# Row gathers of a product-key lookup: six slots and weight units loaded ahead, in place of eight slots

## What is computed

```
q = (xt @ w_q).reshape(T, 8, 2, 128)                 # 8 heads
sc = einsum('thcd,hckd->thck', q, sub_keys)          # 2 x 128 scores a head
s1, i1 = top_k(sc[:, :, 0], 16); s2, i2 = top_k(sc[:, :, 1], 16)
cand = s1[..., :, None] + s2[..., None, :]           # 256 pairs
top_s, top_pos = top_k(cand, 16); gate = softmax(top_s)
idx = take(i1 * 128 + i2, top_pos)                   # 16 experts a token and head
hid = gelu(einsum('tkd,td->tk', u[idx], xt), approximate=False)
out = einsum('tk,tkd->td', gate * hid, v[idx])
```

## Time and profile before

| | |
|---|---|
| three runs, median (lowest to highest) | 2395.85 us (2390.09 to 2397.31) |
| the profiled execution, and its span | 2390.07 us, 2388.0 us |
| TensorE busy | 2096.7 us, 88% |
| VectorE busy | 1732.6 us, 73% |
| ScalarE busy | 789.3 us, 33% |
| GpSimd busy | 574.8 us, 24% |
| moved by DMA | 726.83 MB, mean 304 GB/s |
| granted TensorE clock, mean | 0.985 |
| chain that ended last | DMA 22%, TensorE 23%, VectorE 14%, issue 11% |

### The profile page before, as it was taken

The page is one execution under the profiler, slowest core; times in us unless marked ns, Lnnn a source line. Parts: engine busy times, 40 slices in busy tenths (PEclk is TensorE's granted clock), DMA queues, the critical chain, the costliest instruction groups (busy, mean ns, idle before and its releaser), DMA issues.

```text
span 2388.0 us, 26690 instructions
## 1 busy us (share of the span) xinstructions
PE 2096.7 (88%) x9124; PEld 1365.8 (57%) x9124; DVE 1732.6 (73%) x3737; ACT 789.3 (33%) x1479; POOL 574.8 (24%) x520
## 2 busy tenths in 40 slices
PE   8999999999999889887778779999888988787777
PEld 8998889989877444432322226978544432222224
DVE  6455664558766887878887776656878787878786
ACT  4335653346574221211211116344312121211114
POOL 0000000000101334444444330000434444443430
PEclk9999999999999999999999999999999999999999
DMA  7554325544325999999999995534899999999995
GB/s 264 180 187 168 139 106 179 191 176 168 124 92 192 421 420 416 411 411 420 409 417 416 408 409 220 198 139 172 363 419 420 419 415 419 404 416 420 399 420 209
DMA packets 101354, 726.83 MB, mean 304 GB/s; under 512 B 11632, under 2 KB 11888, under 8 KB 13424
## 3 DMA queue, kind: packets, MB, share of 16 engines
q0 software_dynamic: 74016, 539.00, 54.9%
q1 hardware_dynamic: 25200, 181.41, 21.0%
q10 hardware_dynamic: 2016, 4.89, 0.6%
HBM read 724.21 MB, written 1.05 MB: 304 GB/s over the span
## 4 chain that ended last, share of the span: by engine, by line
PE 23%; DMA 22%; DVE 14%; issue 11%; ACT 2%; POOL 1%; DVEq 0%; POOLq 0%; ACTq 0%
PE bank L2023 23%; DMA arena<-in_uv,expert 22%; DVE arena L1897 3%; DVE arena L1951 2%; POOL arena L677 1%; DVE arena L1870 1%; DVE top_i L1848 1%; DVE arena L1840 1%; DVE top_i L1838 1%; DVE arena L1874 1%; DVE top_v L1843 0%; DVE top_v L1835 0%; DVE sel_s L1851 0%; DVE sel_i L1876 0%; ACT w_hi L730 0%
## 5 line engine op out<-in xcount | busy, mean ns | idle before, releaser
L2023 PE MATMUL bank<-arena 128*128 128x512 f32 (+4 forms) x2416 | 1068.6, 575 | 248.9 <-DVE arena L1897 245.1
L2023 PEld LDWEIGHTS bank<-arena 128*128 128x128 f32 (+2 forms) x2416 | 415.9, 193 | 812.9 <-DVE arena L1897 522.5
L677 POOL DMA_INDIRECT arena<-in_uv,expert x512 | 564.1, 1102 | 1090.1 <-PE bank L2023 657.4
L1951 DVE SCALAR_TENSOR_TENSOR arena<-arena,xn 128x1024 f32<-128x1024 f32 x512 | 626.8, 1224 | 240.3 <-DMA arena<-in_uv,expert 221.5
L1268 DVE TENSOR_TENSOR lw_rounded<-lw,w_hi 128x2048 fp32r<-128x2048 f32 x157 | 362.0, 2306 | 198.6 <-ACT w_hi L730 195.4
L1163 ACT ACTIVATE act_h<-hid 128x1 f32<-128x1 f32 x512 | 103.6, 203 | 1044.5 <-DVE arena L1951 1044.1
L2023 PE MATMUL bank<-xT_hi,w_hi 128*128 128x256 f32 x1320 | 415.5, 315 | 5.5 <-DVE xT_lo L1313 5.5
L730 ACT ACTIVATE w_hi<-lw 128x2048 fp32r<-128x2048 f32 (+1 forms) x177 | 320.7, 1819 | 237.9 <-PE bank L2023 224.0
L2023 PE MATMUL bank<-xT_hi,lw_rounded 128*128 128x256 f32 x1320 | 374.9, 284 | 0.0
L2023 PE MATMUL bank<-xT_lo,w_hi 128*128 128x256 f32 x1320 | 374.7, 284 | 0.0
L2023 PEld LDWEIGHTS bank<-xT_hi,w_hi 128*128 128x128 f32 x1320 | 253.9, 192 | 30.6 <-issue 29.6
(11 more groups left out here) (258 smaller groups left out, 1529.1 us busy)
## 6 DMA issues: line engine op xcount, KB each, us to landing
lw<-in_units SPq DMA_DIRECT2D x169, 1024.0 KB, 4.8
arena<-in_uv,expert POOLq DMA_INDIRECT x512, 12.4
wide<-in_wide POOLq DMA_DIRECT2D x2, 1024.0 KB, 8.9
gain<-in_gains ACTq DMA_DIRECT2D x4, 512.0 KB, 9.4
wide<-in_units SPq DMA_DIRECT2D x2, 1024.0 KB, 7.1
h<-in_x SPq DMA_DIRECT2D x2, 512.0 KB, 4.2
arena<-in_ret_consts ACTq DMA_DIRECT2D x1, 1024.0 KB, 5.2
out<-xn SPq DMA_DIRECT2D x2, 512.0 KB, 2.6
```

Source lines behind the costliest of these rows:

```text
L677: nc.gpsimd.indirect_dma_start(out=rows_uv[:, slot, :], out_offset=None, in_=table, in_offset=bass.IndirectOffsetOnAxis(ap=expert[par][:, ...
L1951: V.scalar_tensor_tensor(rows_uv[:, slot, 0:D], rows_uv[:, slot, 0:D], 1.0, xn[:, tile, :], ALU.mult, ALU.mult, accum_out=hid[par][:, k:k ...
L2023: return nc.tensor.matmul(o, lhsT, rhs, start=start, stop=stop, **more)
```

## The change

SLOTS is 6. The memory of `rows_uv` keeps its eight blocks; in each layer two of them (0 and 1 in the first, 4 and 5 in the second) hold the units head+3 and head+4, the query weights of heads 2 and 3, and the gathers rotate over the other six. These two units are loaded right behind the first query's unit, with semaphores of their own, and their remainder is written in place. The other units keep the ring, but in another order of issue: head+2, head+5, head+7, head+6, head+8, head+9, each behind the unit that held its ring slot before. On VectorE every diagonal follows its own dot, after both top-k steps; AT_ONCE goes. The first six gathers find free slots in place of the first eight.

```
-SLOTS = 8
+SLOTS = 6
+BLOCKS = 8
+UNIT_BLOCKS = ((0, 1), (4, 5))
+ROW_BLOCKS = [[b for b in range(BLOCKS) if b not in blocks] for blocks in UNIT_BLOCKS]
-AT_ONCE = 12
...
-LOADS = {u: sum(v not in WHOLE for v in range(u % RING, u + 1, RING)) for u in range(UNITS)}
+BLOCK_OF = {first + 3 + i: UNIT_BLOCKS[layer][i] for layer, first in enumerate((A_PEER0, A_PEER1)) for i in range(2)}
+LOADS = {u: sum(v not in WHOLE and v not in BLOCK_OF for v in range(u % RING, u + 1, RING)) for u in range(UNITS)}
...
-        rows_uv = region(at, "rows_uv", SLOTS, 2 * D)
+        rows_uv = region(at, "rows_uv", BLOCKS, 2 * D)
+        def row_slot(s):
+            return rows_uv[:, ROW_BLOCKS[s // (ROWS * TOPK)][s % SLOTS], :]
+        def unit_of(u):
+            return rows_uv[:, BLOCK_OF[u], :] if u in BLOCK_OF else lw[:, u % RING, :]
+        def low_of_unit(u):
+            return arena_rounded[:, BLOCK_OF[u] * 2 * D:(BLOCK_OF[u] + 1) * 2 * D] if u in BLOCK_OF else w_lo[:, u % RING, :]
...
                 load_units(head, head + 1, 1)
-                load_units(head + 2, first)
-                sp.wait_ge(row_landed[SLOTS - 3], 16 * (layer + 1) * (ROWS * TOPK // SLOTS))
+                for i in range(2):
+                    sp.dma_start(rows_uv[:, UNIT_BLOCKS[layer][i], :], units_d[head + 3 + i]).then_inc(block_loaded[i], 16)
+                for u, before in ((head + 2, head - 2), (head + 5, head - 3), (head + 7, head - 1), (head + 6, head + 2), (head + 8, head + 1),
+                                  (head + 9, head + 5)):
+                    sp.wait_ge(lw_used, before + 1)
+                    load_unit(u, u % RING)
+                last = (layer + 1) * ROWS * TOPK - 3
+                sp.wait_ge(row_landed[last % SLOTS], 16 * (last // SLOTS + 1))
...
-                            slot = k % SLOTS
+                            s = done + (2 * pair + par) * TOPK + k
                             pool.wait_ge(slot_free, done + SLOTS * layer + (2 * pair + par) * TOPK + k + 1)
-                                out=rows_uv[:, slot, :], out_offset=None, in_=table,
+                                out=row_slot(s), out_offset=None, in_=table,
...
-                            at_once = row == ROWS - 1 and k > AT_ONCE
-                            if at_once:
-                                assert n is None
-                                spread(row * TOPK + k - 1, par, k - 1)
-                            dve.wait_ge(row_landed[slot], 16 * (layer * ROWS * 2 + 2 * row + k // SLOTS + 1))
+                            dve.wait_ge(row_landed[s % SLOTS], 16 * (s // SLOTS + 1))
                             if n is not None:
                                 picked(row + 1, n)
-                            V.scalar_tensor_tensor(rows_uv[:, slot, 0:D], rows_uv[:, slot, 0:D], 1.0, xn[:, tile, :], ALU.mult, ALU.mult,
+                            V.scalar_tensor_tensor(row_slot(s)[:, 0:D], row_slot(s)[:, 0:D], 1.0, xn[:, tile, :], ALU.mult, ALU.mult,
                                                    accum_out=hid[par][:, k:k + 1]).then_inc(dot_done, 1)
                             n = next(ahead, None) if k >= start else None
-                            if k >= 1 and not at_once:
-                                if n is not None:
-                                    picked(row + 1, n)
-                                spread(row * TOPK + k - 1, par, k - 1)
-                                n = next(ahead, None) if k >= start else None
+                            if n is not None:
+                                picked(row + 1, n)
+                            n = next(ahead, None) if k >= start else None
+                            spread(row * TOPK + k, par, k)
                             if k == 10:
                                 weigh(row + 1, 1 - par)
                             beside(slots + par * TOPK + k)
-                        spread(row * TOPK + TOPK - 1, par, TOPK - 1)
...
-                    mm(bank[b][:, :], zeros, consts[:, 0:BANK], True, True).then_inc(slot_free, SLOTS // 4)
+                    mm(bank[b][:, :], zeros, consts[:, 0:BANK], True, True).then_inc(slot_free, (SLOTS + 3 - b) // 4)
```

29 lines of the change are left out of this document (18 added, 11 removed).

## The result

| | before | after |
|---|---|---|
| median of 20 runs each (lowest to highest) | 2392.91 us (2389.16 to 2399.38) | 2398.86 us (2392.22 to 2405.64) |
| ratio | | 1.0019, 95% interval 1.0010 to 1.0028 |
| span of the profiled execution | 2388.0 us | 2393.7 us |

The forecast was 2384.0 us, a gain of 0.5%; what came is no change by the bound of 0.3%, and rather a loss. So some 12 us that I had promised were given back, and 4.5 more (0.0019 x 2393; the two medians alone lie 6.0 us apart).

What follows compares the result with a forecast made beforehand. DMA engines, full in both PEER lookups, were taken as the bound. -14.9 + 3.0 + 0 + 0 = -11.9 us on 2390.07 gave 2378.2; the median's 5.8 us more made 2384.0, own range 2380 to 2388, wide range 2374 to 2400.

Steps and rivals of the forecast that it cites:

- The bound: In the two PEER lookups the DMA engines never rest, and each 1 MiB gather or weight unit costs 2.49 us.
- Part 1: Units loaded ahead: three transfers of 2.49 us leave each lookup, 7.5 us each, -14.9 us over two layers.
- Part 3: Each diagonal behind its own dot: VectorE waits 51 us a layer for the Gelu, covered by idle time; 0 us.
- Part 2, the start: Six slots at each lookup's start: turns 0.6 us over for several gathers, 1.5 us per layer, +3.0 us.
- Part 2, the steady stretch: Six slots through the rest of a lookup: a slot's turn fits into 14.9 us; cost taken as 0.
- the turn of 14.6 us: Worst groups, with a unit's remainder: 3.4 lag + 1.22 + 1.3 + 3.19 + 5.5, fitting 14.9 us by 0.3.
- the late Gelu: At k = 8 the next row's Exp goes first on ScalarE with table loads, making the Gelu 1.3 us late.
- the upper bound: Steady cost of six slots with all delays at once: 1.9 us over in 12 groups, 23 us.
- Rival B: Six slots too few, in the groups carrying a unit's remainder: 1.6 us over gives about 2403, at most 2425; chance 0.10.
- rival C: Table loads holding ScalarE twice 1.28 us make the k = 8 wait 3.9 us: +27, about 2411; chance 0.02.
- A: Gain eaten by lag at the start or groups running over, 8 to 12 us back: 2392; chance 0.20.
- the sign I had named for part 2: If the lookups are not shorter, the six-slot term was wrong; they were forecast some 6 us shorter.

Runs made afterwards that it cites:

- fewer8: Kernel before (eight slots) without the loads of head units +4, +5 and +7 in either lookup, so three heads have wrong queries; 2377.5 us, ratio 0.9940.
- own8: Kernel before with one change: each diagonal follows its own dot, with eight slots and the old loads; 2393.9 us, ratio 1.0007.
- late6: Kernel after with the old order of diagonals, each behind the next row's dot; 2464.8 us, ratio 1.0309 to before.
- hold6: Kernel before with own-dot diagonals and gathers held so that at most six are in flight, eight slots kept in memory; 2406.9 us, ratio 1.0060.
- blocks_late: Kernel after with its unit loads put back to the times of before; 2409.2 us, ratio 1.0076 to before.
- busy6: Kernel after with 3 to 6 products of zeros ahead of TensorE's wait for the diagonal in seven places; 2396.2 us, ratio 1.0012 to before.
- seven: Kernel after with seven slots, one block for unit +4 and two units loaded ahead per lookup; 2385.8 us, ratio 0.9962 to before.
- grow_halves: Kernel after with six, then eight slots from gather 29, a changed ScalarE start order and remainders in halves; 2377.7 us, ratio 0.9936 to before.
- start6: Kernel after with Gelu's table loaded ahead and query 1's copy moved behind the first Gelu; 2398.2 us, ratio 1.0015 to before.

## Why the prediction was wrong, point by point

- **The bound**, DMA engines full in the lookups at 2.49 us a MiB: right (fewer8). Two slips of reading change nothing: the full slices of the earlier trace rows in the lookups run from 399 to 421 and not from 404 to 424, and 111.7 less 51 leaves 60.7 us of cover and not 57.
- **Part 1**, three transfers leave, -14.9 us: right; -14.4 with eight slots, -13.6 with six, issue times as forecast.
- **Part 3**, own-sum diagonals, 0: right at eight slots (own8, +1.7, interval -0.5 to +3.8), and the wait on act_h has about the size forecast (51 us a layer by my sum, 119.5 in both). What I did not see is the other side: with six slots the old order would have cost 69 us more (late6).
- **Part 2, the start**, +3.0 us: groups 0 and 1 of after exceed fewer8's by 3.8 and 1.6 us in the two lookups, 5.4 together. Mis-sized, within its bounds (0 to 6.6).
- **Part 2, the steady stretch**, "I take 0, since the terms are seen apart and not together": this step failed. From group 2 on, after exceeds fewer8 by 3.2 and 6.2 us in the profiled executions (14.8 us with the start), and all in all six slots cost 12.7 (hold6) to 18.9 us (after against fewer8, own-sum's 1.7 included). Two terms of the turn of 14.6 us were wrong. "Issue to landing at least 5.5" should have been 8.0, the lead at which the stream holds; with it the same worst slot comes to 17.1 us of 14.9. And the late Gelu was put at 1.3 us, where ScalarE is 4.3 us late once a layer, at the first tile's Sqrt. I had the ingredients for the upper bound (23 us, which held), and chose the lower end because each delay was seen alone. But they need not meet: 14.9 less (1.22 + 0.27 + 3.19 + 8.0) leaves 2.2 us, and one remainder of 2.29 us on VectorE fills that.
- **Rival B** (six slots too few) had the cause, and part of the place: remainders cut in halves return 6.5 us, but group 8, with 5.8 us over fewer8 in the two lookups together, carries no remainder. Its chance of 0.10 was too low. Of rival C only the k = 8 was right: it is a third table load at group 8, not a drain. The result lies between the prices of A (2392) and B (2403 for 1.6 us over), so it falls into the wide range of 2374 to 2400 for A's and B's sake and not for the forecast's; "within 0.3%" had a chance of 0.22.
- Of the signs: the median landing (9.2), the waits and the issues on SP came out as forecast, and the lookup was 1.9 us longer instead of 6 shorter, which is the sign I had named for part 2.

What stays open: what the remainders cost at eight slots, whether the start's order and TensorE's lighter work gain up to 3 us, why blocks_late costs 3.8 us more than hold6 (intervals overlap, so perhaps nothing), and how large the clock's share is in the whole (busy6, 1.7 us, not told from nothing).

## What to carry to other kernels

A buffer's turn has to be reckoned with the time that a transfer needs in a full stream (here 8.0 us from issue to landing), not with the shortest one in the trace; and the reserve that is left must hold the longest single operation that can stand in front of the consumer, on each engine that the turn passes. Memory borrowed from a rotation for the start of a stage can be given back within it: six slots at first and eight from gather 29 on kept 10.5 of the 14.4 us (all of them with the remainders in halves and the start's order), where six throughout lost them. Where DMA is the bound, read GB/s against its best stretch: the busy share stayed at 1.00 while 7.9 us of 300 were lost.

## What the runs showed of the hardware

- **One beat in about 18 is 3.46 us instead of 2.49**, in every kernel and without any lag: in the quiet part of after gathers 180, 198, 216 and 234 land 3.45 us behind the one ahead of them. It makes the 1.0 per group in the tables, some 13 us a lookup. The traces show what goes with it. Take the landings of gathers 160 to 249 in both lookups of before, and the interval ahead of each. In 13 of them the DMA engines also moved an 8 KiB packet that the profile books as an instruction's (q14), and 9 of these are over 3.2 us; of the 167 others none is. In own8, seven and grow_halves it is the same (9 or 10 with, none without). In each of before's nine, one packet of a gather took over 0.9 us, where the median packet takes 0.31. The DMA view of before, 1194.7 to 1198.2, gather 161:

```profile
q14 instruction: 1, 0.01, 0.6%
```

So the loss goes with the loading of instructions beside a full stream. No run changed that loading, so the cause isn't shown.
- **TensorE's clock falls inside a stage that is 0.98 to 0.99 on the whole**: behind idle times of 2.0 to 3.7 us in seven places of after the matmuls took 1.06 us instead of 0.59. Idle time alone doesn't foretell it: behind four idle times of 3.0 us in after and one of 3.65 in start6 they took 0.59. With short products of zeros in front and 1.4 to 2.3 us idle, six of the seven places kept 0.59 in busy6. Before has more slow matmuls than after (38 and 15 of over 0.8 us in its two lookups, 20 and 9 in after's), so the clock doesn't make the difference between the two; with eight slots no late landing goes with them in the quiet part.
- **Descriptor generation** (POOL's DMA_INDIRECT) takes 0.94 us alone and up to 1.9 beside VectorE's dots. With the own-sum order its mean rose from 1102 ns in before to 1238 ns in own8 and 1222 in after. In after, gathers that overlap two-input operations of VectorE for under 0.3 us take 0.94 us in the mean (97 of them), those that overlap 1.3 us or more 1.79 (55). At eight slots it costs nothing. The Trainium skill, SBUF — State Buffer, section Who interferes with whom, says that a VectorE instruction with two SBUF inputs contends with a GpSimd instruction that reads SBUF, not with one that only writes it. The gather's row numbers stand in SBUF, so the longer times beside such instructions fit the sentence, though no run here separated reads from writes.
